# Unread transposes of the identity on TensorE around the transposes of the first expert rows

## What is computed

```python
logits = t @ w_router + b_router
top_val, top_idx = lax.top_k(logits, TOP_K)          # TOP_K = 4 of 32
gate = softmax(top_val)
# tokens sorted by expert, padded to chunks of 128 rows; one chunk = one expert
gu = xc @ w_gate_up[e] + b_gate_up[e]                # xc: 128 x 1024
g = minimum(gu[:, :1024], 7.0); u = clip(gu[:, 1024:], -7.0, 7.0)
act = (u + 1.0) * (g * sigmoid(1.702 * g))
y = act @ w_down[e] + b_down[e]
out = zeros(n, d).at[slot_tok].add(y * slot_w)
```

## Time and profile before

| | us |
|---|---|
| median of 3 runs | 2040.78 |
| lowest, highest | 2039.48, 2044.6 |
| the profiled execution, its own time | 2039.13 |
| its span, first to last instruction | 2037.5 |
| busy: PE, DVE, ACT, POOL | 1953.8, 1564.4, 1280.0, 291.9 |
| mean granted clock of TensorE | 0.983 |

### The profile page before, as it was taken

How to read it: one execution, slowest core, us unless ns; L and a number is a source line. 1 busy time by engine, 2 the same in 40 slices (tenths; PEclk the granted TensorE clock), 3 DMA queues, 4 the chain that set the end, 5 groups by cost and what they waited for, 6 DMA issues and landing times.

```text
span 2037.5 us, 36966 instructions
## 1 busy us (share of the span) xinstructions
PE 1953.8 (96%) x11706; PEld 1520.2 (75%) x11707; DVE 1564.4 (77%) x2025; ACT 1280.0 (63%) x1772; POOL 291.9 (14%) x350
## 2 busy tenths in 40 slices
PE   7999999999996999999999999999999999999993
PEld 6777778888685777777777778877778877777783
DVE  4788855566657879788777779977879988976896
ACT  5555555454534767667666568756667767755775
POOL 3100000000135211102211110211111101211110
PEclk8999999999997999999999999999999999999997
DMA  5030111011445978989887799979889989888995
GB/s 185 21 104 1 41 43 42 21 42 42 155 189 171 331 264 298 373 296 371 290 281 270 268 362 374 334 268 358 298 291 374 379 289 370 314 276 292 377 372 194
DMA packets 256288, 489.99 MB, mean 240 GB/s; under 512 B 20194, under 2 KB 38478, under 8 KB 256144
## 3 DMA queue, kind: packets, MB, share of 16 engines
q1 hardware_dynamic: 233824, 439.56, 59.8%
q0 software_dynamic: 21376, 49.81, 9.0%
q10 hardware_dynamic: 1040, 0.00, 0.0%
HBM read 461.66 MB, written 32.18 MB: 242 GB/s over the span
## 4 chain that ended last, share of the span: by engine, by line
PE 88%; DVE 5%; issue 2%; ACT 2%; DMA 1%; POOL 1%; POOLq 0%; ACTq 0%; SPq 0%; DVEq 0%
PE psum L836 17%; PE psum L837 17%; PE psum L840 17%; PE psum L849 8%; PE psum L513 3%; PE psum L515 3%; PE psum L514 3%; PE psum L646 3%; PE psum L650 3%; PE psum L648 3%; PE psum L822 3%; PE psum L796 1%; PE psum L866 1%; PE psum L769 1%; PE psum L770 1%
## 5 line engine op out<-in xcount | busy, mean ns | idle before, releaser
L1917 DVE TENSOR_TENSOR w_lo<-ring,w_hi 128x1024 fp32r<-128x1024 f32 x768 | 908.8, 1221 | 98.0 <-ACT w_hi L1197 87.1
L1197 ACT ACTIVATE w_hi<-ring 128x1024 fp32r<-128x1024 f32 x768 | 789.6, 1058 | 126.1 <-PE psum L840 120.0
L836 PE MATMUL psum<-w_hi,rows_hi 128*128 128x512 f32 x1024 | 425.9, 416 | 0.0
L837 PE MATMUL psum<-w_hi,rows_lo 128*128 128x512 f32 x1024 | 400.3, 391 | 0.0
L840 PE MATMUL psum<-w_lo,rows_hi 128*128 128x512 f32 x1024 | 316.3, 390 | 0.0
L840 PEld LDWEIGHTS psum<-w_lo,rows_hi 128*128 128x128 f32 x1024 | 192.8, 188 | 41.4
L837 PEld LDWEIGHTS psum<-w_hi,rows_lo 128*128 128x128 f32 x1024 | 193.4, 189 | 38.2
L836 PEld LDWEIGHTS psum<-w_hi,rows_hi 128*128 128x128 f32 x1024 | 194.0, 189 | 36.6
L836 PE MATMUL psum<-w_hi,act_hi 128*128 128x512 f32 x512 | 215.2, 420 | 0.0
L837 PE MATMUL psum<-w_hi,act_lo 128*128 128x512 f32 x512 | 199.8, 390 | 0.5 <-issue 0.5
L849 PE MATMUL psum<-ring,region_m 128*32 128x256 f32 x3072 | 171.9, 379 | 0.0
(11 more groups left out here) (373 smaller groups left out, 3009.4 us busy)
## 6 DMA issues: line engine op xcount, KB each, us to landing
ring<-in_w_gate_up_dram SPq DMA_DIRECT2D x128, 2048.0 KB, 17.8
ring<-in_w_down_dram SPq DMA_DIRECT2D x64, 2048.0 KB, 12.8
ring<-in_w_in_dram SPq DMA_DIRECT2D x16, 512.0 KB, 5.1
region_m<-in_x_dram SPq DMA_DIRECT2D x8, 512.0 KB, 9.4
ring<-in_w_in_dram SPq DMA_DIRECT2D x2, 2048.0 KB, 15.7
ring<-in_w_out_dram SPq DMA_DIRECT2D x2, 2048.0 KB, 7.8
region_a<-in_x_dram POOLq DMA_DIRECT2D x8, 512.0 KB, 5.2
acc_rows<-region_a POOLq DMA_DIRECT2D x8, 512.0 KB, 3.7
```

What stands on the lines that cost most here:

```text
L836: mm(bank(i), hi[:, ks], wh, start=False, stop=False)
L837: mm(bank(i), lo[:, ks], wh, start=False, stop=False)
L1197: act.activation(w_hi[:, n % NBUF, :], place[i][:, k0 * HALF:(k0 + 2) * HALF], ACT.Copy).then_inc(hi_done, 1)
L1917: v.tensor_tensor(out=w_lo[:, n % NBUF, :], in0=place[i][:, k0 * HALF:(k0 + 2) * HALF], in1=w_hi[:, n % NBUF, :].bitcast(f32), op=ALU.subt ...
```

## The change

A function `keep_warm(n)` issues n transposes of the identity `ident` into bank 3 of PSUM; no instruction reads what they write. It is called twice: with 10 between line 809's products and the wait for `rows_in`, and with 16 behind `rows_turn`, ahead of the wait for the step table.

```diff
@@ -796,6 +796,10 @@
                     last = tr(bank(6, 2)[:, k * P:(k + 1) * P], rows_g[:, k * P:(k + 1) * P], ident[:])
                 last.then_inc(rowsT_mm, 1)
 
+            def keep_warm(n):
+                for _ in range(n):
+                    tr(bank(3)[:, 0:P], ident[:], ident[:])
+
             pe.sem_inc(sub_mm, NBUF)
             pe.sem_inc(tgate_mm)
             pe.sem_inc(tup_mm)
@@ -808,8 +812,10 @@
             for s in range(NT):
                 last = mm(bank(5)[:, 2:5], first_hot[:, s, :], first_w[:, s, 0:3], start=(s == 0), stop=(s == NT - 1))
             last.then_inc(count_mm, 1)
+            keep_warm(10)
             pe.wait_ge(rows_in, 16)
             rows_turn()
+            keep_warm(16)
             pe.wait_ge(table_done, 1)
             total = pe.value_load(ends[0:1, 0:1], min_val=1, max_val=MAXS)
             pe.wait_ge(bias_done, 3)
```

## The result

| | us |
|---|---|
| before, median of 5 runs (lowest, highest) | 2040.95 (2039.48, 2044.6) |
| changed, median of 5 runs (lowest, highest) | 2048.54 (2047.87, 2052.04) |
| ratio, 95% interval | 1.0039 (1.0024 to 1.0054) |
| profiled execution of the changed kernel, its span | 2052.04, 2050.4 |

The change costs 0.39%, 7.6 us between the medians, where I had forecast none and given a slowdown of over 0.3% two chances in a hundred. The profiled execution is the slowest of the five, so a part of its 12.9 us over the one of before is scatter: 5.4 of them are there before the first product of the down projection (693.32 instead of 687.89), 6.2 come between it and the second step, 1.3 behind that.

The account below looks back on a forecast made before the run. PE's own work was taken as the bound (busy 96% of the span); +0.56 us (rows late), -2.6 (cold stretch gone) and +2.0 (absorbed at two floors) gave 0, so 2040.1 us, range 2037.5 to 2043.

Parts of the forecast that it names:

- 8, "Instructions": 52 added instructions in PE's stream ahead of the step count and table reads: taken as 0, without cover 0 to 0.5 us.
- A fetch of code: Half-way case: the clock rises later or fetching code adds some tenths, between -0.5 and +0.5 us; chance 0.04.
- Step 1: Price of one filler transpose, start to start: 0.221 us at 1.2 GHz, 0.114 us at 2.4 GHz.
- Step 2: Ten fillers behind line 809 take 2.2 us; rows' transposes start 0.56 us late, first expert matmul moves from 661.16 to 661.72.
- Step 3: Sixteen fillers from 659.05 end at 662.6 cold or 660.9 warm; first expert matmul at 661.72 (`rows_lo`) or 662.6 (fillers).
- Step 4: PE's clock rises at 658.9 to 660.3 us, within the sixteen fillers, so the expert loop starts warm at 661.72.
- The first rival: No warming: identity transposes do not raise the clock, fillers delay the expert loop to 662.6; +0.1, 2040.2 us, chance 0.12.
- Step 5: First two pieces of the expert loop at full instead of half clock: PE reaches the same point 2.0 us ahead.
- Step 6: The 2.0 us lead is lost in the first expert step, at waits for `act_lo` and the next rows' gather; gain 0.
- The floor that took the lead: First of two floors independent of PE: weight landings hold ACT and DVE, so `act_lo` holds PE's down projection at 687.89.
- Slower: Prefetch collides: next expert's load, issued some 2 us sooner, delays step 1's table and gather; at most 2042.2 us, chance 0.10.

Follow-up runs that it names:

- the block of 246: Never-entered code at the start of PE's program moves the expert loop by 246 instructions in all: kernel before 1.0004, 2045.54 us; changed kernel with fillers 1.0002, 2045.62 us.
- sixteen behind alone: Changed kernel with `keep_warm(10)` left out, so only the sixteen transposes behind the rows' (32 instructions): 1.0023 of the kernel before, 2049.45 us.
- the block of 256: Never-entered code at the start of PE's program moves the expert loop by 256 instructions in all: kernel before 1.0007, 2045.76 us; changed kernel with fillers 1.0018, 2047.68 us.
- the last pair of runs: Kernel before and changed kernel, each with never-entered code moving the expert loop by 246 instructions in all: 1.0004, 2045.54 us without fillers; 1.0002, 2045.62 us with them.
- the pair at 256: Kernel before and changed kernel, each with never-entered code moving the expert loop by 256 instructions in all: 1.0007 without fillers, 1.0018 with them.
- the pair at 246: Kernel before and changed kernel, each with never-entered code moving the expert loop by 246 instructions in all: 1.0004 without fillers, 1.0002 with them.
- the seven traces of the table without a block: Kernel before twice, ten transposes ahead 1.0010, seven wide products for the transposes 1.0017, sixteen behind 1.0023, the change 1.0039, 52 semaphore increments instead of fillers 1.0032.
- ten ahead: Changed kernel with `keep_warm(16)` left out, so only the ten transposes ahead of the rows' (20 instructions): 1.0010 of the kernel before, 2048.57 us.

## Why the prediction was wrong, point by point

- **The step that failed is 8, "Instructions".** I saw that 52 instructions come into PE's stream, asked only for the time to issue them, took 0 and gave 0 to 0.5 us as the bound. The term is +5.5 us of gap less the 0.5 that was there, and behind it the cold stretch: 4 us of work at half clock from 699.2 to 703.2, 2 us more. That is 7 us; the medians show 7.6, and the time from the bias to the second step 20.30 instead of 14.11 (6.2, as the 0.42 us of wait for the next rows are gone). The row that should have warned me stands in PE's waits of before, "issue", 0.5 us, in the down projection at full DMA; I read it as waiting for nobody and left it out of the rows. A fetch of code was among the rivals with "some tenths" and 0.04.
- **Step 1** held: ten fillers in 2.37 us, pace (2.37-0.42)/9 = 0.217. **Step 2**, 0.56 us of delay, did not happen in this execution: the rows came at 659.60, 2.9 us later than in the earlier trace rows, and PE stood idle 0.96 us behind the ten.
- **Step 3** took the wrong end. The first expert product comes 5.17 us behind the rows' transposes (664.77-659.60), against 4.44 before; I had said 4.44 with 5.3 as the other end. The sixteen and not `rows_lo` set the start. In the three other runs with sixteen it is 4.97 to 4.99.
- **Step 4**, the clock, came late, and in other runs just in time. In the changed kernel all sixteen show 0.421 us, and the window 665.5 to 666.0 has the first 0.88; I had expected 658.9 to 660.3. With fillers and the block of 246 the sixteen took 3.39 instead of 3.62 us and the bias behind them, at 666.38, 0.38 instead of 0.58, so there the clock was up although PE had done nothing but transposes since 657.98. With sixteen behind alone the last fillers themselves run at full pace, ahead of the bias at 664.35, and PE had been idle for 3.37 us ahead of the rows' eight at 659.38:

```profile
L801 PE MATMUL psum<-ident x16: 272/418/418, 661.1 to 664.2; 128*128 128x128 f32 x16
```

  The first rival, that turned identity does not count, falls with that, and so does for this place the rule of the Trainium skill, TensorE: Matmul & The Clock Gate, Part 4 (PE-mode transpose), that transposes do not count as busy for the clock.
- **Step 5** held in the main: from the first product to piece 4 it is 8.12 us before (669.28-661.16) and 6.10 after, with the block of 256 8.29 without fillers and 5.71 with them, with the block of 246 7.19 and 5.67. Net of the later start that is a lead of 1.3, 2.0 and 1.0 us (I said 2.0).
- **Step 6** held in the outcome, not in the place, as the last pair of runs shows: the lead ends in PE's wait for `w_hi`, which is 4.3 us with fillers and 2.3 without, at equal times. I had put it into the wait for `act_lo`, which should have grown by 1.5 to 2 us; it is 0.82 in the changed kernel against 0.91. The floor that took the lead is the landing of unit 2's weights, which I had named as the first.
- **The rivals.** Slower came true, but not by my rival for it: the next rows' transposes at 707.27 followed without any wait for the gather, so the prefetch collided with nothing that mattered. The wait that took the place was one for code.

Open stays, besides what starts the fetch, why it takes 6 us. The queues are full at the time (1.05), and the packet itself appears some 3 us into the gap, which suggests waiting in line behind weights; no run here lightened the DMA to see. Open is also whether the fillers cost up to 0.1%: the pair at 256 says so, the pair at 246 does not. And no version beats the kernel before: with the boundary 10 instructions later the time to step 2 is 1.0 to 1.4 us shorter (12.72 against 13.70 and 14.11), and the kernel with the block that moves it is still at 1.0004.

## What to carry to other kernels

Instructions that are added to an engine with a long unrolled program move all the code behind them, and in the first pass through a loop this alone can cost more than what they execute. Before a change is judged, look in the engine's waits for "issue" in the first pass, count how many instructions lie between that place and the last blocking wait or jump over code, and compare with a control that moves the code by as much and runs nothing. If the boundary lies badly, shift it behind the point with most queued work.

## What the runs showed of the hardware that I had not expected

- PE's instructions arrive by DMA in 16 KB packets, at fixed places in the stream: the gap stood at PE's 6563rd record in the seven traces of the table without a block, whatever code was there, and with a block of 256 at the old place of the code again. In the loop's first pass at full DMA PE resumed 5.7 to 6.5 us after the wait in front, 1.3 to 1.6 us after the packet had landed. In later steps the same places show no gap: from the second step on all kernels take 1335 to 1337 us.
- An idle stretch of 5.5 us in the middle of dense float32 work brought the clock from 1.00 to 0.50, and PE worked another 4 us before it was back. One of 3.07 us (ten ahead) left it at 1.00.
- A semaphore increment on PE took 0.15 us from start to start (52 of them from 647.9 to 655.7), although each is shown with 0.051.
